# Copying the turned probabilities of memory pairs with VectorE in place of ScalarE, in layer 0's prompt attention

## The chip, the core and the metric

One core of a Trainium2 chip runs the whole program. Its engines are TensorE (PE in the profile, with its weight loads as PEld), VectorE (DVE), ScalarE (ACT), GpSimd (POOL) and SyncE (SP, which here only issues the loads of weights). Each engine works through its own list of instructions in order; they wait for each other through semaphores. The metric is the time of one execution in microseconds (us).

## What is computed

The reference is one step of a two-layer decoder for a prompt of 1,024 tokens and a sample group of 8 x 4 tokens. What matters here is the attention of layer 0 over the prompt, which has two parts that share one output projection:

```
# sliding window: 12 query heads on 4 key/value heads, blocks of 128 queries, 256 keys (own block and the one before)
s = einsum(q, k) * 64**-0.5 - slope * dist         # masked outside the window
m = max(max(s), sink);  e = exp(s - m)
p = e / (sum(e) + exp(sink - m));  o = einsum(p, v)
# memory: 4 heads, every query on 256 memory tokens, no bias
s = einsum(xq, mk) * 64**-0.5
p = softmax(s);  xo = einsum(p, mv)
x = x + concat([o, xo]) @ w_out
```

Layer 1 has the same memory attention, and a gated mixer in place of the window.

## The kernel before

All activations lie in SBUF with features on partitions and the 1,056 tokens along the free dimension. Most of the program is projections in which each fp32 product is split into three (lines 449 to 451); weights stream in through `raw`, are split by ScalarE and GpSimd, and TensorE is never long without work there.

The change concerns `prompt_attention(0)`, a stage of its own between the sample attention and the output projection. Its work is a list of 48 items: for each of 8 blocks of 128 queries four window items, called g0 to g3 here (three heads each, on a shared key/value head), and two memory items, m0 and m1 (a pair of heads each). An item passes through these steps:

- scores (PE, L645): 3 or 2 matmuls of 256 keys into two PSUM banks, which alternate between items.
- top (DVE): for a window item, three bias additions that also copy the scores to `s_exp` (L1424), a maximum (L1430) and two tiny operations on the sink (L1433, L1436); for a memory item only a maximum straight from PSUM (L1440).
- exps (ACT, L1014 and L1017): the exponentials with their sums.
- scale: the reciprocal of the sum on DVE (L1449 and L1452, or L1454), then a multiplication on POOL (L419).
- turn (PE, L659): transposes of the probabilities into PSUM banks 4 and 5, 6 or 4 of 128 x 128.
- take: one copy of these from PSUM to `p_t` in SBUF, 768 columns wide for a window item (384 in block 0) and 512 for a memory item. It is recorded at L850, the line of the helper `scopy` on ScalarE.
- values (PE, L672 for window items, L678 for memory items): the products with v.
- high (ACT, L850) and low (DVE, L1460): the split of the output into its high part `h_hi` and the rest, `h_lo`.

What sets the order is the loop `for n in range(...)` that each engine has, with LAG = 3. In turn n, TensorE does scores(n), turn(n-3), values(n-4). ScalarE does take(n-3), high(n-4), exps(n). VectorE does low(n-5), top(n), scale(n-1). Banks 4 and 5 are not doubled: turn(n) waits until take(n-1) is done (`pturned_taken`). `p_t` is doubled: take(n) waits for values(n-2) (`pv`). So m0 and m1 of a block are turned, and their probabilities taken, in the turns that do the scores of g1 and g2 of the next block; the last two are taken after the last scores. The wait that ties the engines most closely is this one, in TensorE's `turn`:

```
pe.wait_ge(m["normed"], n + 1)
if n >= 1:
    pe.wait_ge(m["pturned_taken"], n)
```

Of the kernel before, what the change touches and what calls it, by code (L numbers as in the profile page):

```python
# [64 lines left out]
LAG = 3  # L65
# [44 lines left out]
def swa_items(layer):  # L110

    out = []
    for b in range(NB):
        if layer == 0:
            out += [("swa", b, g) for g in range(A_KV)]
        out += [("mem", b, p) for p in range(2)]
    return out


def hybrid_step(nc, d, o, slopes):  # L120
    ctx = ExitStack()
    with ctx:
# [8 lines left out]
        def put(name, shape, dt=F32):  # L131
            t = nc.alloc_sbuf_tensor_at(name, shape, dt, offset=cursor[0])
            cursor[0] += size(shape)
            return t
# [80 lines left out]
        p_t = put("p_t", [P, 2, 2 * 3 * P])  # L215
# [45 lines left out]
        def banks(b, n, width):  # L261
            return ps[:, b:b + n, :].rearrange("p b n -> p (b n)")[:, 0:width]
# [585 lines left out]
        def _(act):  # L848
            def scopy(out, in_):
                return act.activation(out, in_, ACT.Copy)  # L850
# [145 lines left out]
            def prompt_attention(l):  # L996
                m = mx[l]
                items = swa_items(l)
                se, pt, st = (s_exp, p_t, stat) if l == 0 else (s_exp1, p_t1, stat1)
                N = len(items)  # L1000
                if l == 0:

                    act.wait_ge(outs, 16 * n_out[0])

                def exps(n):
                    kind, b, g = items[n]
                    act.wait_ge(m["ready"], n + 1)
                    if kind == "mem" and n >= RING:
                        act.wait_ge(m["pturned"], n - RING + 1)
                    w = BLOCK if kind == "swa" and b == 0 else 256  # L1010
                    for hh in range(3 if kind == "swa" else 2):
                        dst = se[:, n % RING, hh * 256:hh * 256 + w]
                        src = dst if kind == "swa" else ps[:, 2 * (n % 2) + hh, 0:w]
                        ins = act.activation(dst, src, ACT.Exp, bias=st[:, n % 4, 1, hh:hh + 1],  # L1014
                                             accum_out=st[:, n % 4, 2, hh:hh + 1])
                    if kind == "swa":
                        ins = act.activation(st[:, n % 4, 4, :], st[:, n % 4, 3, :], ACT.Exp)  # L1017
                    ins.then_inc(m["exped"], 1)

                def take(n):  # L1020
                    kind, b, g = items[n]
                    nh = 3 if kind == "swa" else 2
                    w = nh * P * (1 if kind == "swa" and b == 0 else 2)
                    act.wait_ge(m["pturned"], n + 1)
                    if n >= 2:
                        act.wait_ge(m["pv"], n - 1)
                    scopy(pt[:, n % 2, 0:w], banks(4, 2, 768)[:, 0:w]).then_inc(m["pturned_taken"], 1)

                def high(n):
                    act.wait_ge(m["pv"], n + 1)  # L1030
                    dst, src = o_view(items[n], n, h_hi)
                    scopy(dst, src).then_inc(m["o_cut"], 1)

                for n in range(N + LAG + 2):
                    if 0 <= n - LAG < N:
                        take(n - LAG)
                    if 0 <= n - LAG - 1 < N:
                        high(n - LAG - 1)
                    if n < N:
                        exps(n)  # L1040
                    if l == 1 and n < NB + 1:

                        w, t0 = (TS, 0) if n == 0 else (BLOCK, TS + (n - 1) * BLOCK)
                        act.wait_ge(m["gate_mult"], n + 1)
                        scopy(h_hi[:, 0:6, t0:t0 + w], z[:, 0:6, t0:t0 + w]).then_inc(m["gate_cut"], 1)
# [75 lines left out]
            for l in range(2):  # L1121
                m = mx[l]
# [63 lines left out]
                if l == 1:  # L1186
                    for n in range(NB + 1):
# [4 lines left out]
                        scopy(vn_tok[0:w, n % 2, :], banks(0, 2, 768)[0:w]).then_inc(m["gate_taken"], 1)  # L1192
                sample_attention(l)
                prompt_attention(l)

                if l == 1:
# [44 lines left out]
        def _(dve):  # L1241
# [45 lines left out]
            for r in range(N_MEMU):  # L1287
                l, q = r // 4, r % 4
# [115 lines left out]
            def prompt_attention(l):  # L1404
                m = mx[l]
                items = swa_items(l)
                se, st = (s_exp, stat) if l == 0 else (s_exp1, stat1)
                N = len(items)
                sums = [0, 0]

                def top(n):
                    kind, b, g = items[n]
                    s4 = n % 4
                    dve.wait_ge(m["scored"], n + 1)
                    out = banks(2 * (n % 2), 2, 768)
                    if n >= 4:
                        dve.wait_ge(m["normed"], n - 3)
                    if kind == "swa":
                        if n >= RING:

                            dve.wait_ge(m["pturned"], n - RING + 1)
                        w, nd0 = (BLOCK, BLOCK) if b == 0 else (256, 0)
                        for j in range(3):
                            STT(out=se[:, n % RING, j * 256:j * 256 + w], in0=nd_p[:, nd0:nd0 + w],  # L1424
                                scalar=float(slopes[3 * g + j]), in1=out[:, j * 256:j * 256 + w],
                                op0=ALU.mult, op1=ALU.add).then_inc(m["biased"], 1)
                        sums[0] += 3
                        dve.wait_ge(m["biased"], sums[0])
                        src = se[:, n % RING, :].rearrange("p (j k) -> p j k", j=3)[:, :, 0:w]
                        dve.tensor_reduce(st[:, s4, 0, :], src, AX, ALU.max, negate=True).then_inc(m["maxed"], 1)  # L1430
                        sums[1] += 1
                        dve.wait_ge(m["maxed"], sums[1])
                        TT(st[:, s4, 1, :], st[:, s4, 0, :], nsink_p[:, 3 * g:3 * g + 3], ALU.min) \  # L1433
                            .then_inc(m["maxed2"], 1)
                        dve.wait_ge(m["maxed2"], sums[1])
                        TT(st[:, s4, 3, :], st[:, s4, 1, :], nsink_p[:, 3 * g:3 * g + 3], ALU.subtract) \  # L1436
                            .then_inc(m["ready"], 1)
                    else:
                        src = ps[:, 2 * (n % 2):2 * (n % 2) + 2, 0:256]
                        dve.tensor_reduce(st[:, s4, 1, 0:2], src, AX, ALU.max, negate=True).then_inc(m["ready"], 1)  # L1440

                swas = [0]

                def scale(n):
                    kind, b, g = items[n]
                    s4 = n % 4
                    dve.wait_ge(m["exped"], n + 1)
                    if kind == "swa":
                        TT(st[:, s4, 0, :], st[:, s4, 2, :], st[:, s4, 4, :], ALU.add).then_inc(m["summed"], 1)  # L1449
                        swas[0] += 1  # L1450
                        dve.wait_ge(m["summed"], swas[0])
                        dve.reciprocal(st[:, s4, 5, :], st[:, s4, 0, :]).then_inc(m["recip"], 1)  # L1452
                    else:
                        dve.reciprocal(st[:, s4, 5, 0:2], st[:, s4, 2, 0:2]).then_inc(m["recip"], 1)  # L1454

                def low(n):
                    dve.wait_ge(m["o_cut"], n + 1)
                    dst, src = o_view(items[n], n, h_lo)
                    hi, _ = o_view(items[n], n, h_hi)
                    TT(dst, src, hi.bitcast(F32), ALU.subtract).then_inc(m["o_done"], 1)  # L1460

                for n in range(N + LAG + 2):
                    if 0 <= n - LAG - 2 < N:
                        low(n - LAG - 2)
                    if n < N:
                        top(n)
                    if 0 <= n - 1 < N:
                        scale(n - 1)
                    if l == 1 and 1 <= n < NB + 2:

                        w, t0 = (TS, 0) if n == 1 else (BLOCK, TS + (n - 2) * BLOCK)
                        dve.wait_ge(m["gate_cut"], n)
                        TT(h_lo[:, 0:6, t0:t0 + w], z[:, 0:6, t0:t0 + w], h_hi[:, 0:6, t0:t0 + w].bitcast(F32),
                           ALU.subtract).then_inc(m["gate_done"], 1)
# [129 lines left out]
            for l in range(2):  # L1604
                m = mx[l]
# [229 lines left out]
```

## Time and profile before

| | before |
|---|---|
| time, median of 3 runs | 2440.69 us |
| the three runs | 2440.69, 2440.61, 2445.96 us |
| span of the profiled execution | 2437.8 us |
| prompt attention of layer 0 in it | about 290 to 441.5 us |
| PE busy | 2364.8 us, 97% |
| DVE busy | 1152.4 us, 47% |
| ACT busy | 674.6 us, 28% |
| POOL busy | 596.1 us, 24% |

The span is what the profiler saw between the first and the last instruction; the time of a run has a few us around it (the median is 2.9 us above the span; the profiled execution's own time is not listed apart). Matmuls are pipelined and their ends are modelled, so that a busy TensorE is one that has something in flight. In a timeline row the first number is the start in us from the beginning of the span, the second the length; the square bracket at the end tells how long the engine sat idle before, and who released it.

### The profile page before, as it was taken

How to read it: one execution, taken by the hardware profiler on the slowest of the kernel's cores; microseconds unless marked ns; L12 is line 12 of the kernel's file. 1: busy time of each engine (PE TensorE's matmuls, PEld its weight loads, DVE VectorE, ACT ScalarE, POOL GpSimd, SP SyncE). 2: the span in 40 equal slices, each digit the busy share in tenths (PEclk: the TensorE clock that was granted, in tenths of full speed). 3: DMA queues.
4: the chain of work that ended last, by engine and by line, in shares of the span. 5: the costliest groups of instructions: out<-in, count | busy, mean ns of one | idle time of the engine just before them, and what ended most of it. 6: DMA issues, size and time to landing. Idle time of an engine off the chain costs nothing.

```text
span 2437.8 us, 37784 instructions
## 1 busy us (share of the span) xinstructions
PE 2364.8 (97%) x14538; PEld 2238.3 (92%) x14538; DVE 1152.4 (47%) x2144; ACT 674.6 (28%) x1247; POOL 596.1 (24%) x413
## 2 busy tenths in 40 slices
PE   5999999999999999999999998899999999999999
PEld 5898755899999999999999997699999999999999
DVE  7213377245454455554455133415555445445554
ACT  6211277242211112222225222514222221112221
POOL 3111033342212122222224121333222221212221
PEclk9998799999999999999999998899999999999999
DMA  5213000111111111111111112011111111111112
GB/s 202 86 44 139 5 1 1 29 44 61 44 43 35 42 47 48 52 52 52 43 35 51 44 44 95 4 43 35 52 53 52 52 43 43 35 42 44 50 52 84
DMA packets 36288, 123.29 MB, mean 51 GB/s; under 512 B 5264, under 2 KB 9968, under 8 KB 34896
## 3 DMA queue, kind: packets, MB, share of 16 engines
q1 hardware_dynamic: 26208, 95.43, 12.7%
q10 hardware_dynamic: 10000, 26.76, 2.9%
q8 instruction: 54, 0.88, 0.2%
q14 instruction: 26, 0.21, 0.0%
HBM read 115.57 MB, written 8.63 MB: 51 GB/s over the span
## 4 chain that ended last, share of the span: by engine, by line
PE 87%; DVE 5%; issue 4%; ACT 2%; POOL 1%; ACTq 0%; DMA 0%; DVEq 0%; POOLq 0%
PE ps L449 26%; PE ps L450 26%; PE ps L451 25%; PE ps L645 2%; DVE h_lo L1258 2%; PE ps L672 2%; PE ps L578 1%; PE ps L659 1%; PE ps L610 1%; ACT s_exp L1014 1%; DVE z L1645 1%; PE ps L722 1%; PE ps L560 1%; ACT p_t L850 0%; DVE s_exp L1424 0%
## 5 line engine op out<-in xcount | busy, mean ns | idle before, releaser
L449 PE MATMUL ps<-h_hi,w_hi 128*128 128x352 f32 x3120 | 1012.7, 325 | 14.9 <-DVE h_lo L1258 5.6
L450 PE MATMUL ps<-h_lo,w_hi 128*128 128x352 f32 x3120 | 1001.5, 321 | 0.0
L451 PE MATMUL ps<-h_hi,w_lo 128*128 128x352 f32 x3120 | 1000.7, 321 | 0.0
L356 POOL TENSOR_TENSOR w_lo<-raw,w_hi 128x1024 fp32r<-128x1024 f32 x138 | 345.1, 2502 | 1497.3 <-ACT w_hi L850 1497.3
L449 PEld LDWEIGHTS ps<-h_hi,w_hi 128*128 128x128 f32 x3120 | 586.3, 188 | 36.5 <-issue 22.3
L450 PEld LDWEIGHTS ps<-h_lo,w_hi 128*128 128x128 f32 x3120 | 587.2, 188 | 0.0
L451 PEld LDWEIGHTS ps<-h_hi,w_lo 128*128 128x128 f32 x3120 | 585.9, 188 | 0.0
L1565 DVE TENSOR_TENSOR x<-x,ps 128x352 f32<-128x352 f32 x528 | 270.7, 519 | 173.9 <-PE ps L451 173.1
L449 PE MATMUL ps<-g_hi,d_hi 128*128 128x352 f32 x1056 | 340.4, 322 | 3.5 <-DVE g_lo L1558 3.5
L450 PE MATMUL ps<-g_lo,d_hi 128*128 128x352 f32 x1056 | 339.9, 322 | 0.0
L451 PE MATMUL ps<-g_hi,d_lo 128*128 128x352 f32 x1056 | 339.7, 322 | 0.0
L850 ACT ACTIVATE w_hi<-raw 128x1024 fp32r<-128x1024 f32 x138 | 144.8, 1051 | 443.5 <-PE ps L451 430.2
L449 PEld LDWEIGHTS ps<-g_hi,d_hi 128*128 128x128 f32 x1056 | 198.3, 188 | 4.0 <-issue 4.0
L451 PEld LDWEIGHTS ps<-g_hi,d_lo 128*128 128x128 f32 x1056 | 198.7, 188 | 0.0
L450 PEld LDWEIGHTS ps<-g_lo,d_hi 128*128 128x128 f32 x1056 | 198.4, 188 | 0.0
L850 ACT ACTIVATE g_hi<-g_f 128x352 fp32r<-128x352 f32 x132 | 64.1, 498 | 443.5 <-DVE g_f L1552 443.5
L1619 DVE TENSOR_TENSOR z<-ps,rb 128x352 f32<-128x352 f32 x78 | 40.1, 523 | 236.0 <-PE ps L451 217.4
L1491 DVE SCALAR_TENSOR_TENSOR c_buf<-a_buf,conv_c,c_buf 128x1024 f32<-128x1024 f32 x88 | 150.3, 1708 | 2.8
L1552 DVE TENSOR_TENSOR g_f<-c_buf,ps 128x352 f32<-128x352 f32 x132 | 66.4, 518 | 165.4 <-PE ps L451 163.2
L1538 DVE TENSOR_TENSOR a_buf<-ps,rb 128x352 f32<-128x352 f32 x88 | 45.8, 524 | 208.0 <-PE ps L451 208.0
L419 POOL TENSOR_SCALAR s_exp<-s_exp,stat 128x256 f32<-128x256 f32 (+1 forms) x160 | 78.7, 507 | 223.7 <-DVE stat L1452 122.0
L356 POOL TENSOR_TENSOR d_lo<-raw,d_hi 128x1024 fp32r<-128x1024 f32 x44 | 106.6, 2422 | 67.9 <-ACT d_hi L850 67.9
(175 smaller groups left out, 1897.0 us busy)
## 6 DMA issues: line engine op xcount, KB each, us to landing
raw<-in_w SPq DMA_DIRECT2D x182, 512.0 KB, 3.6
x<-in_x_t ACTq DMA_DIRECT2D x4, 1056.0 KB, 10.0
out_y<-x ACTq DMA_DIRECT2D x8, 528.0 KB
s_mk<-in_s_mk ACTq DMA_DIRECT2D x2, 2048.0 KB, 9.5
s_mv<-in_s_mv ACTq DMA_DIRECT2D x2, 2048.0 KB, 14.6
mem_x<-in_mem_t ACTq DMA_DIRECT2D x1, 1024.0 KB, 7.0
s_k<-in_s_k ACTq DMA_DIRECT2D x2, 512.0 KB, 4.4
s_v<-in_s_v ACTq DMA_DIRECT2D x1, 1024.0 KB, 17.1
```

The source lines that it names most:

```text
L356: pool.tensor_tensor(lo, raw[:, slot], hi.bitcast(F32), ALU.subtract).then_inc(prepped, 1)
L419: ins = pool.tensor_scalar(v, v, st[:, n % 4, 5, hh:hh + 1], 1.0, ALU.mult, ALU.mult)
L449: pe.matmul(out, a, hi_x(k), start=(first and n == 0), stop=False)
L450: pe.matmul(out, a, lo_x(k), start=False, stop=False)
L451: ins = pe.matmul(out, b, hi_x(k), start=False, stop=(last and n == len(ks) - 1))
L645: mm = pe.matmul(out[:, hh * step:hh * step + w], lhs, rhs, start=True, stop=True)
L672: mm = pe.matmul(ps[64 * half:64 * half + 64, 6 + n % 2, 0:384], v_tok[:, b - len(kcs) + 1 + kc, g * HD:(g + 1) * HD], pt[:, n % 2, kc * 3 ...
L850: return act.activation(out, in_, ACT.Copy)
L1258: STT(out=h_lo[:, k, cs], in0=x[:, k, cs], scalar=gain[:, g_i, k:k + 1], in1=h_hi[:, k, cs].bitcast(F32), op0=ALU.mult, op1=ALU.subtract). ...
L1491: ins = STT(out=cp, in0=ab[:, 48 + j:48 + j + SEQ], scalar=cc[:, j:j + 1], in1=cp, op0=ALU.mult, op1=ALU.add)
L1552: TT(g_f[:, c * CH:(c + 1) * CH], c_buf[:, s, c * CH:(c + 1) * CH], ps[:, 3 + c, 0:CH], ALU.mult).then_inc(freed[1], 1)
L1565: TT(xx, xx, ps[:, 3 + (q + 1) % 5, 0:CH], ALU.add).then_inc(dn_added, 1)
```

## The change

In layer 0 the 16 takes of memory items leave ScalarE and are done by VectorE with `tensor_copy`, with the same two waits and the same signal. Those of window items, and all of layer 1, stay. ScalarE's loop skips them; VectorE's loop has them as the last step of a turn: low(n-5), top(n), scale(n-1), take(n-3).

```diff
@@ ScalarE, prompt_attention
                 for n in range(N + LAG + 2):
-                    if 0 <= n - LAG < N:
+                    if 0 <= n - LAG < N and (l == 1 or items[n - LAG][0] == "swa"):
                         take(n - LAG)
@@ VectorE, prompt_attention
+                def take(n):
+                    dve.wait_ge(m["pturned"], n + 1)
+                    if n >= 2:
+                        dve.wait_ge(m["pv"], n - 1)
+                    dve.tensor_copy(p_t[:, n % 2, 0:512], banks(4, 2, 768)[:, 0:512]).then_inc(m["pturned_taken"], 1)
...
                         top(n)
                     if 0 <= n - 1 < N:
                         scale(n - 1)
+                    if l == 0 and 0 <= n - LAG < N and items[n - LAG][0] == "mem":
+                        take(n - LAG)
```

VectorE's order in a block, before: top of g1 (four rows), the scale of g0 (L1449, L1452), then low of the g3 of the block before (L1460), and the beginning of top of g2.

```order
L1424 SCALAR_TENSOR_TENSOR s_exp<-nd_p,ps 128x256 x3
L1430 TENSOR_REDUCE stat<-s_exp 128x3
L1433 TENSOR_TENSOR stat<-stat,nsink_p 128x3
L1436 TENSOR_TENSOR stat<-stat,nsink_p 128x3
L1449 TENSOR_TENSOR stat<-stat 128x3
L1452 RECIPROCAL stat<-stat 128x3
L1460 TENSOR_TENSOR h_lo<-ps,h_hi 64x3x128
L1424 SCALAR_TENSOR_TENSOR s_exp<-nd_p,ps 128x256 x3
L1430 TENSOR_REDUCE stat<-s_exp 128x3
L1433 TENSOR_TENSOR stat<-stat,nsink_p 128x3
```

The same place of VectorE in the changed program, where line numbers behind the new function are higher by 6 (L1430 is L1424 of before, L1458 is L1452, L1466 is L1460) and L1415 is the new copy:

```order
L1430 SCALAR_TENSOR_TENSOR s_exp<-nd_p,ps 128x256 x3
L1436 TENSOR_REDUCE stat<-s_exp 128x3
L1439 TENSOR_TENSOR stat<-stat,nsink_p 128x3
L1442 TENSOR_TENSOR stat<-stat,nsink_p 128x3
L1455 TENSOR_TENSOR stat<-stat 128x3
L1458 RECIPROCAL stat<-stat 128x3
L1415 COPY p_t<-ps 128x512
L1466 TENSOR_TENSOR h_lo<-ps,h_hi 64x3x128
L1430 SCALAR_TENSOR_TENSOR s_exp<-nd_p,ps 128x256 x3
```

The copy for m0 stands between the reciprocal of g0 and low of g3; the copy for m1 stands one turn later in the same way, between the reciprocal of g1 and low of m0. ScalarE at the same place, before and then changed, where p_t<-ps is a take and h_hi<-ps a high:

```order
L1017 ACTIVATE stat<-stat 128x3
L850 ACTIVATE p_t<-ps 128x512
L850 ACTIVATE h_hi<-ps 64x3x128
L1014 ACTIVATE s_exp,stat<-s_exp,stat 128x256 x3
L1017 ACTIVATE stat<-stat 128x3
L850 ACTIVATE p_t<-ps 128x512
L850 ACTIVATE h_hi<-ps 128x128
```

```order
L1017 ACTIVATE stat<-stat 128x3
L850 ACTIVATE h_hi<-ps 64x3x128
L1014 ACTIVATE s_exp,stat<-s_exp,stat 128x256 x3
L1017 ACTIVATE stat<-stat 128x3
L850 ACTIVATE h_hi<-ps 128x128
```

On ScalarE both takes are gone, and what stood around them now stands side by side. TensorE's order is the same in both programs.

## Rows read from the trace of the kernel before

**Rows 1.** The page, part 1: each engine's busy time, share of the span, instructions.

```profile
PE 2364.8 (97%) x14538; PEld 2238.3 (92%) x14538; DVE 1152.4 (47%) x2144; ACT 674.6 (28%) x1247; POOL 596.1 (24%) x413
```

**Rows 2.** Busy time by stage: layer 0's prompt attention, and two us of layer 1's.

```profile
core 0: us, PE busy (x) PEld busy (x) DVE busy (x) ACT busy (x) POOL busy (x), PEclk, DMA share, GB/s
292.00:440.00 148.00, 144.57 (x730) 83.88 (x732) 109.32 (x328) 115.71 (x383) 57.90 (x128) 0.97 0.00 1
1552.00:1554.00 2.00, 1.56 (x16) 0.86 (x14) 1.74 (x4) 2.00 (x8) 1.57 (x2) 1.00 0.05 12
```

**Rows 3.** Costliest groups, shapes apart, from 290 to 442 us.

```profile
L1440 DVE TENSOR_REDUCE stat<-ps 128x2 f32<-128x512 f32 x16 | 10.8, 678 | 0.1
...
L850 ACT ACTIVATE p_t<-ps 128x512 f32<-128x512 f32 x16 | 9.5, 596 | 0.7 <-PE ps L659 0.3
```

**Rows 4.** The same view over the whole span: VectorE reads of PSUM and SBUF.

```profile
L1619 DVE TENSOR_TENSOR z<-ps,rb 128x352 f32<-128x352 f32 x78 | 40.1, 523 | 236.0 <-PE ps L451 217.4 <-ACT rb L850 18.7
...
L1396 DVE COPY o_s<-ps 64x32 f32<-64x32 f32 x8 | 1.5, 189 | 25.0 <-PE ps L610 24.9
...
L1320 DVE COPY s_k<-z 128x256 f32<-128x256 f32 x2 | 0.5, 289 | 0.0
```

**Rows 5.** Timeline, prompt block 3, 363 to 375 us (start, length, engine, instruction).

```profile
363.63 1.08 DVE L1424 SCALAR_TENSOR_TENSOR s_exp<-nd_p,ps 128x256 f32<-128x256 f32 x3 [0.42 <-PE ps L645]
...
366.20 0.18 DVE L1452 RECIPROCAL stat<-stat 128x3 f32<-128x3 f32 x1
366.41 0.56 DVE L1460 TENSOR_TENSOR h_lo<-ps,h_hi 64x384 fp32r<-64x384 f32 x1
...
367.03 0.66 PE L659 MATMUL ps<-ident,s_exp 128*128 128x128 f32 x4
...
367.14 1.08 DVE L1424 SCALAR_TENSOR_TENSOR s_exp<-nd_p,ps 128x256 f32<-128x256 f32 x3 [0.17 <-PE ps L645]
...
367.86 0.60 ACT L850 ACTIVATE p_t<-ps 128x512 f32<-128x512 f32 x1
...
369.63 0.51 ACT L1014 ACTIVATE s_exp<-s_exp,stat 128x256 f32<-128x256 f32 x1 [1.00 <-DVE stat L1436]
...
369.70 0.87 PE L659 MATMUL ps<-ident,s_exp 128*128 128x128 f32 x6
369.71 0.18 DVE L1452 RECIPROCAL stat<-stat 128x3 f32<-128x3 f32 x1
369.80 0.26 DVE L1460 TENSOR_TENSOR h_lo<-ps,h_hi 128x128 fp32r<-128x128 f32 x1
...
369.98 1.07 DVE L1424 SCALAR_TENSOR_TENSOR s_exp<-nd_p,ps 128x256 f32<-128x256 f32 x3
...
372.16 0.84 PE L659 MATMUL ps<-ident,s_exp 128*128 128x128 f32 x6 [0.36 <-ACT p_t L850]
...
374.06 0.79 ACT L850 ACTIVATE p_t<-ps 128x768 f32<-128x768 f32 x1
...
375.00 0.88 PE L659 MATMUL ps<-ident,s_exp 128*128 128x128 f32 x6
```

**Rows 6.** Timeline, prompt block 1, 309 to 319 us.

```profile
309.54 0.18 DVE L1452 RECIPROCAL stat<-stat 128x3 f32<-128x3 f32 x1
...
310.34 1.08 DVE L1424 SCALAR_TENSOR_TENSOR s_exp<-nd_p,ps 128x256 f32<-128x256 f32 x3
...
313.18 1.07 DVE L1424 SCALAR_TENSOR_TENSOR s_exp<-nd_p,ps 128x256 f32<-128x256 f32 x3
...
318.20 0.87 PE L659 MATMUL ps<-ident,s_exp 128*128 128x128 f32 x6
```

**Rows 7.** Timeline, end of the stage and the first matmul of the output projection.

```profile
439.13 0.56 DVE L1460 TENSOR_TENSOR h_lo<-ps,h_hi 64x384 fp32r<-64x384 f32 x1 [1.69 <-ACT h_hi L850]
439.20 0.60 ACT L850 ACTIVATE p_t<-ps 128x512 f32<-128x512 f32 x1
...
441.52 0.42 PE L449 MATMUL ps<-h_hi,w_hi 128*128 128x352 f32 x1 [1.01 <-DVE h_lo L1460]
```

**Rows 8.** Line 659, transposes on TensorE: duration in ns, minimum/median/maximum.

```profile
L659 PE MATMUL ps<-ident,s_exp x308: 272/273/474, 295.1 to 1573.7; 128*128 128x128 f32 x154
```

## The prediction

> **What bounds the kernel now.** Begin with the engines' shares [rows 1]: TensorE has work in flight for 97% of the span, so a change can shorten the program only where TensorE waits, and lengthens it where it makes TensorE wait. Next the stage [rows 2]: in the 148 us of layer 0's prompt attention TensorE is busy for 144.6, ScalarE for 115.7, VectorE for 109.3. Neither helper is full, and ScalarE is the fuller one; by these sums alone the move looks harmless. The sums don't say who is late at which moment, so the timeline of one block comes next [rows 5]. The blocks repeat every 18.93 us from block 2 to block 7; the rows are of block 4. What to see in them:
>
> - TensorE turns m0's successor m1 at 367.03, g0 at 369.70, g1 at 372.16 and g2 at 375.00. Its only idle time of note is 0.36 us before 372.16, for ScalarE's take of g0. Before 375.00 it is on the edge too: ScalarE's take of g1 ends at 374.06 + 0.79 = 374.85, and the turn starts 0.15 later.
> - ScalarE takes m1 at 367.86, then still sits idle for 1.00 us before its exponentials of g2 at 369.63, until VectorE has finished top of g2.
> - VectorE idles 0.42 us before top of g1 (363.63) and 0.17 us before top of g2 (367.14), both times for TensorE's scores. From 367.14 on it goes through top of g2, the reciprocal at 369.71, low of m0 at 369.80 and top of g3 at 369.98 without a pause.
>
> So in the middle of a block the chain runs VectorE (top), ScalarE (exponentials, then the take behind them), TensorE (turn). VectorE leads it. In this stretch the engine that receives the copies is the one that is late, and the one that gives them up is waiting for it.
>
> **What is removed.** Sixteen ScalarE copies of 596 ns [rows 3], 9.5 us of work. Both of a block lie ahead of an idle time: exponentials of g2 can't start before VectorE's top, whatever ScalarE has to do before. Removing 0.60 us from in front of 1.00 us of waiting gains nothing. If it did gain, only TensorE's 0.36 us per block could be won back.
>
> **What is added: the length of one copy.** No row shows VectorE copying 512 fp32 columns from PSUM. The nearest: a maximum over 512 columns from PSUM takes 678 ns [rows 3]; an addition with a 352-column PSUM operand takes 523 ns and a copy of 32 columns 189 ns [rows 4], a slope of (523 - 189) / 320 = 1.044 ns a column, which gives 189 + 480 x 1.044 = 690 ns. The other end: the copy from SBUF to SBUF of 256 columns takes 289 ns [rows 4], that is 100 ns for 224 columns more than 32, or 0.45 ns each; at such a rate 512 columns would take 189 + 480 x 0.45 = 405 ns. I take 690, since it rests on two kinds of PSUM reads and the maximum lies within 12 ns of it, and keep 405 and, for waits that no row prices, 760 as the ends.
>
> The Trainium skill bears on this choice ("VectorE: DVE Perf Modes"). Its tier table allows `tensor_copy` up to two results a cycle from PSUM, which would put it near the short end, while its section "Why PSUM operands drop a tier" says one for fp32, since VectorE has one PSUM read port; no row here shows a wide copy from PSUM. Its cycle table, 120 + 512 cycles at 0.96 GHz, gives an estimate of 658 ns, and the sum below would come out 0.5 us lower by it.
>
> **What is added: the shift, in a steady block.** Take m0: it is ready (turned before 365), so it starts when VectorE gets to it. In the rows an instruction can start 0.09 us after the start of a reciprocal (369.71, 369.80), so the copy runs from 366.20 + 0.09 = 366.29 to 366.98. TensorE's turn of m1 needs it and moves from 367.03 to some 367.1, which is covered by waits further on. Low of g3 moves from 366.41 to 367.01 (it writes the other half of the partitions, and at 366.41 it too started only once its forerunner had ended), ends at 367.57, and top of g2 starts at 367.60 in place of 367.14: **0.46 later**, the copy less the small idle times in front of it.
>
> Take m1: VectorE reaches it after top of g2 and the reciprocal, at 369.80 + 0.46 = 370.26, and ends at 370.95. ScalarE did it at 367.86. TensorE's turn of g0 needs it, and moves from 369.70 to 370.95 + 0.15 = 371.10, **1.40 later**; this is the new wait, and queued behind it on TensorE stand values of m1, the scores of m0 and the turn of g1. Low of m0 and top of g3 follow the copy; as an independent instruction starts 0.08 before its forerunner's end (low of m0 ends at 370.06, the next starts at 369.98), the copy costs 0.61 in the queue, and top of g3 moves by 0.46 + 0.61 = **1.07**, to 371.05.
>
> What of it reaches the end of the block? Along TensorE: from the turn of g0 to that of g1 it has 372.16 - 369.70 - 0.36 = 2.10 of work and from there to the turn of g2 2.84, so that the turn of g2 could stand at 371.10 + 2.10 + 2.84 = 376.04, 1.04 later. The take of g0 doesn't add to this: it is ready 0.9 after the turn began and is over before 373.2. Along VectorE and ScalarE: top of g3, its exponentials and the take of g1 keep their distances, so the take ends at 374.85 + 1.07 = 375.92 and the turn stands at 376.07, **1.07 later**. The later of the two holds. Behind the turn of g2 comes TensorE's stretch without waits, and at the next block's top of g1 VectorE waits for TensorE again (0.42 us), so that nothing is left over or piled up. POOL's multiplications move with the reciprocals and are over before their turns, as now. No DMA is issued in the stage's loop, and the weight buffers are full while it runs.
>
> **The first block and the end.** Block 1 is the first to do this, and in it VectorE has no idle time ahead of top of g2: it starts at 310.34, right behind low [rows 6]. The copy for m0 would run from 309.63 to 310.32, low starts at 310.35, 0.60 late, and top of g3 (313.18) moves by 0.60 + 0.61 = 1.21, with it the turn of g2 at 318.20. Blocks 2 to 7 are six steady ones. At the end, low of the last g3 ends at 439.69 and ScalarE's take of the last m1 runs from 439.20 to 439.80 [rows 7]; VectorE can start it at 439.72 only and ends at 440.41, 0.61 later, and the output projection's first matmul (441.52) waits for values, high and low behind it.
>
> **The sum.** 6 x 1.07 + 1.21 + 0.61 = 8.24 us. All of it shifts a program that is TensorE's work from there on. The span goes from 2437.8 to 2446.0, and with the 2.9 us by which the median of the runs lies above the span, the median from 2440.7 to **2448.9**, 0.34% more.
>
> **The rivals.**
>
> *The copy is short.* It decides in the same place: with 0.405 in place of 0.690 the shift of top of g3 is 2 x 0.285 = 0.57 less in each of seven blocks, and the end 0.29 less, together 4.3 us less: 2444.6 us, which is not slower by 0.3%. The point from which it decides: 0.3% is 7.3 us (about what a measurement of this kernel can tell from no change), which needs a copy of about 0.63 us, since each 0.01 us costs 0.15. For it speaks the SBUF copy's rate [rows 4], against it every wide read of PSUM. Chance 0.12.
>
> *ScalarE was the one that was late.* If the copies hid in VectorE's idle time and ScalarE's relief counted, TensorE's waits for the take of g0 would go: 0.36 x 7, with the first block's about 3 us. That gives 2437.7 us, which is faster but within 0.3%. Against it stands the 1.00 us that ScalarE waits for VectorE [rows 5]. Chance 0.03.
>
> *The clock of TensorE falls.* It is granted in full here (0.97 of 2.4 GHz over the stage), and the new wait leaves TensorE without work for 1.3 us in every block. At the lower level a transpose takes 474 ns in place of 273 [rows 8], 1.74 times; one block of 18.6 us of work there would cost up to 14 us, 2463 us in all. Against it: in layer 1's attention TensorE is busy for 1.56 us of 2, and the clock stays full [rows 2]. Chance 0.02.
>
> *The mechanism holds with another size.* Should VectorE's two added waits cost 0.07 each (copy 0.76), it is 9.3 us; should the instructions overlap by 0.08 more at low of g3, 7.7 us. These are the bounds of my own case, 0.83.
>
> **How the numbers follow.** Of my own case's 0.83 I put 0.66 above 7.3 us, as its centre lies only 0.9 above. With the clock's 0.02, slower has 0.68. The rest of my case, the short copy and most of ScalarE's case make 0.30 for within 0.3%; faster keeps 0.02. The range leaves out the clock's case, the gain and a little of the short copy's side: 2444.6 to 2451.5, where 1.5 us at the upper end is for the spread between runs.
>
> **What would show it.** In the changed profile: the copy of `p_t` on VectorE 16 times at 0.69 us; TensorE idle some 1.3 us before one turn in each block, released by VectorE's copy, and no longer 0.36 for the take of g0; the blocks 20.0 us apart in place of 18.93; ScalarE's busy time 9.5 us lower and VectorE's 11 higher; the output projection starting at 449.8. I am wrong if the copy takes about 0.4, if the period stays at 18.9 (the copies hidden), or if the transposes of this stage show 474 ns.

## The result, and the profile after

The change makes the kernel slower: 2454.57 us against 2440.65, a ratio of 1.0056 with a 95% interval of 1.0042 to 1.0070, or 13.9 us. The prediction had 8.2 us and a range up to 2451.5, so the time came out later than the whole range: the direction is right and the size is not. (The two medians rest on four runs each; later runs of both kernels, below, spread more than these did.)

The span of the profiled execution is 2453.1 us, 15.3 more than before. The page's engine row (busy us, share of the span, instructions) answers to [rows 1]:

```profile
PE 2371.7 (97%) x14538; PEld 2244.5 (91%) x14538; DVE 1163.6 (47%) x2160; ACT 667.9 (27%) x1231; POOL 596.6 (24%) x413
```

VectorE has 16 instructions and 11.2 us more, ScalarE 16 and 6.7 us less. TensorE has the same instructions and 6.9 us more busy time, which is the first hint: no wait makes a matmul longer. ScalarE's busy time fell by less than the 9.5 us forecast because a copy overlaps its neighbours on the engine: the 0.60 us copy at 367.86 in [rows 5] still runs when ScalarE's next instruction starts at 368.36.

The timeline of block 3 answers to [rows 5], whose rows are of block 4, as the prediction says and not its caption; the steady blocks are alike (line numbers behind the new function are 6 higher, and the clock stayed full in block 3 of this profile):

```profile
351.06 1.08 DVE L1430 SCALAR_TENSOR_TENSOR s_exp<-nd_p,ps 128x256 f32<-128x256 f32 x3 [0.42 <-PE ps L645]
...
353.64 0.18 DVE L1458 RECIPROCAL stat<-stat 128x3 f32<-128x3 f32 x1
353.73 0.68 DVE L1415 COPY p_t<-ps 128x512 f32<-128x512 f32 x1
...
354.44 0.56 DVE L1466 TENSOR_TENSOR h_lo<-ps,h_hi 64x384 fp32r<-64x384 f32 x1
354.55 0.63 PE L659 MATMUL ps<-ident,s_exp 128*128 128x128 f32 x4
355.03 1.08 DVE L1430 SCALAR_TENSOR_TENSOR s_exp<-nd_p,ps 128x256 f32<-128x256 f32 x3
...
357.53 0.51 ACT L1014 ACTIVATE s_exp<-s_exp,stat 128x256 f32<-128x256 f32 x1 [1.42 <-DVE stat L1442]
...
357.69 0.68 DVE L1415 COPY p_t<-ps 128x512 f32<-128x512 f32 x1
358.29 0.28 DVE L1466 TENSOR_TENSOR h_lo<-ps,h_hi 128x128 fp32r<-128x128 f32 x1
358.48 1.07 DVE L1430 SCALAR_TENSOR_TENSOR s_exp<-nd_p,ps 128x256 f32<-128x256 f32 x3
358.52 0.84 PE L659 MATMUL ps<-ident,s_exp 128*128 128x128 f32 x6 [1.25 <-DVE p_t L1415]
```

Everything stands where the prediction put it. Counted from top of g1, top of g2 starts 3.97 us later, where it started 3.51 later before (+0.46); the turn of g0 starts at 7.46 in place of 6.07 (+1.39) behind an idle time of 1.25 us that VectorE's copy ends; top of g3 starts at 7.42 in place of 6.35 (+1.07). ScalarE's wait for top of g2 has grown from 1.00 to 1.42 us: its relief went into waiting.

One block later the same turn looks different. Timeline of block 4, the copy and TensorE behind it, then windows over the same time (columns: busy us and count, granted clock, DMA share, GB/s):

```profile
377.65 0.68 DVE L1415 COPY p_t<-ps 128x512 f32<-128x512 f32 x1
378.48 1.28 PE L659 MATMUL ps<-ident,s_exp 128*128 128x128 f32 x6 [1.25 <-DVE p_t L1415]
380.75 1.22 PE L645 MATMUL ps<-mem_k,z 64*128 64x256 f32 x4
```

```profile
376.00:378.00 2.00, 1.23 (x6) 1.00 0.00 0
378.00:380.00 2.00, 1.52 (x10) 0.68 0.04 12
380.00:382.00 2.00, 2.00 (x13) 0.50 0.00 0
382.00:384.00 2.00, 2.00 (x10) 0.96 0.00 0
```

The six transposes take 1.28 us in place of 0.84. Some 0.3 us into them the clock falls from 2.4 to 1.2 GHz and comes back 3.4 us later. What TensorE did before it fell: it stood idle for 1.25 us, and was busy before and after. The same happens in blocks 1, 4 and 6, and once more right after the stage, where TensorE had waited for the last copy (0.71 us) and, after 0.7 us of work, for the last high and low (1.01 us). With the tops of g1 as marks, the stage is:

| | before | after |
|---|---|---|
| first scores of the stage | 288.5 | 292.0 |
| from there to top of g0, block 1 | 15.6 | 14.8 |
| top of g1, block 1, to top of g1, block 2 | 18.77 | 21.39 |
| the same for blocks 2 to 6 | 18.93 or 18.94 | 19.97, 19.97, 21.41, 19.96, 21.38 |
| top of g1, block 7, to the output projection | 21.09 | 22.75 |
| first scores to the output projection | 153.0 | 164.5 |

The 15.3 us of the span are thus: 3.5 before the stage, where nothing was changed; 11.5 in the stage; 0.3 behind it (the output projection took 1.5 us more there, and the profile before had a stretch at 1.2 GHz of its own, from 561.4 us, that this one lacks). The 11.5 are 8.0 of added waiting (1.04 in each of six steady blocks, 1.2 in block 1, 0.6 at the end), 4.3 for three blocks that are 1.43 us longer, and 0.8 less before the first copy, as the clock there came back to its full level sooner after the stage's start.

### The profile page after: what moved, and what is told of

It is laid out like the page before. It is cut to its first block, busy times and chain, and to the rows that moved or that the text cites. A ratio compares the mean times of both kernels' runs of the same rounds, so it can differ in the third digit from the quotient of the medians.

```text
span 2453.1 us, 37784 instructions
## 1 busy us (share of the span) xinstructions
PE 2371.7 (97%) x14538; PEld 2244.5 (91%) x14538; DVE 1163.6 (47%) x2160; ACT 667.9 (27%) x1231; POOL 596.6 (24%) x413
## 4 chain that ended last, share of the span: by engine, by line
PE 86%; DVE 6%; issue 4%; ACT 2%; POOL 1%; ACTq 0%; DVEq 0%; POOLq 0%
PE ps L449 26%; PE ps L450 25%; PE ps L451 25%; DVE h_lo L1258 2%; PE ps L645 2%; PE ps L672 1%; PE ps L578 1%; PE ps L659 1%; PE ps L610 1%; DVE s_exp L1430 1%; DVE stat L1436 1%; DVE z L1653 1%; PE ps L722 1%; PE ps L560 1%; ACT s_exp L1014 0%
```

## Experiments

The questions: do the two copies make the 8.0 us, each in its place? What are the blocks with the lower clock, and the 3.5 us ahead of the stage?

**The kernel before and the changed kernel, again.** No edit.

> The kernel before, unchanged, for a second profile of it. In the profile after the change the stage begins 3.5 us later than in the one of before (292.0 against 288.5 us), though nothing in front of it is changed: TensorE's clock stood at its lower level over other stretches. Theory A (those stretches come with the program and return with it): the stage begins at 288.5 again, within 0.3 us, the same stretches show the lower clock, ratio to the kernel before 1.000. Theory B (they come by chance with each execution): the stage begins anywhere within some 3 us of that, and the lower clock lies elsewhere. In both the stage itself, first scores to first matmul of the output projection, takes 153.0 us within 1, with no lower clock after its first 14 us.

> The changed kernel, unchanged, for a second profile of it. In the first one the stage takes 164.5 us against 153.0 and shows three stretches of 3.4 us at the lower clock (from 317, 379 and 420 us), each of which made its block 1.4 us longer; my sum of waits had 8.2 us. Theory A (the stretches return with the program): the same three blocks, stage 164.5 us, start at 292.0. Theory B (the new wait opens the door to them, chance decides which blocks): again one to seven such stretches, in other blocks, stage 160 to 170 us. Theory C (they have nothing to do with the change): none, stage 161 us. In all, blocks without such a stretch are 19.97 us apart (18.93 before).

Before, again: median 2442.39 of 11 runs, ratio 1.0001 [0.9990, 1.0011]. The stage began at 291.6, not at 288.5, and took 152.2 us, its blocks 18.94 apart, with no lower clock in blocks 1 to 7. After, again: 2454.09 of 5 runs, ratio 1.0052 [1.0033, 1.0071]. The stage began at 289.6 and took 162.3 us; block 5 alone was longer (21.34), the others 19.94 to 19.97. Theory B holds and A falls: the stretches don't come with the program. The 3.5 us ahead of the stage are chance, and single times of either kernel spread by many us: 2438.7 to 2447.2 before, 2446.2 to 2459.0 after. The added waiting was the same in both profiles of the changed kernel.

**Half of the change.**

```diff
 # m0_only (m1_only with 0 and 1 exchanged)
-                    if 0 <= n - LAG < N and (l == 1 or items[n - LAG][0] == "swa"):
+                    if 0 <= n - LAG < N and (l == 1 or items[n - LAG][0] == "swa" or items[n - LAG][2] == 1):
                         take(n - LAG)          # ScalarE
...
-                    if l == 0 and 0 <= n - LAG < N and items[n - LAG][0] == "mem":
+                    if l == 0 and 0 <= n - LAG < N and items[n - LAG][0] == "mem" and items[n - LAG][2] == 0:
                         take(n - LAG)          # VectorE
```

> Half the change: only the copy of m0 goes to VectorE, m1's stays on ScalarE. By my sum of waits: top of g2 moves by 0.46 us in a steady block and the turn of g2 with it, 0.60 in block 1, nothing at the end: blocks 19.39 us apart, the stage longer by 0.60 + 6 x 0.46 = 3.4 us without any clock effect. TensorE's wait ahead of g0's turn (1.25 us with the whole change) isn't there; it has two short ones instead, below 0.9. If the lower clock comes with the long wait, there is none of it here in blocks 2 to 7, and the ratio is about 1.0014. If it has nothing to do with that wait, some blocks show it, 1.4 us each.

> The other half: only the copy of m1 goes to VectorE. It starts at once behind the reciprocal of g1: turn of g0 0.94 us late, top of g3 0.60 late and with it the turn of g2: blocks 19.53 us apart, the stage longer by 7 x 0.60 + 0.61 = 4.8 us without clock effect; TensorE waits about 0.9 us ahead of g0's turn. The two halves together (3.4 + 4.8) make the 8.2 of the whole change if the mechanism is additive. If a wait of 0.9 us is long enough for the lower clock, one or more blocks are 1.4 us longer in addition; if it takes the 1.25 of the whole change, none is.

Copy of m0 alone: blocks 19.39 apart, the stage behind top of g0 of block 1 at 140.8 us against 137.4 to 137.5 in the two profiles of before (+3.3), ratio 1.0008 [0.9996, 1.0020]. The copy of m1 alone: 19.51 apart, 142.15 (+4.7), ratio 1.0038 [1.0023, 1.0054]. 3.3 and 4.7 make the 8.0 of the whole. The turn that waits, in the timelines of m0_only and then of m1_only:

```profile
355.92 0.85 PE L659 MATMUL ps<-ident,s_exp 128*128 128x128 f32 x6 [0.75 <-ACT p_t L850]
```

```profile
315.77 0.68 DVE L1415 COPY p_t<-ps 128x512 f32<-128x512 f32 x1
316.60 0.85 PE L659 MATMUL ps<-ident,s_exp 128*128 128x128 f32 x6 [1.50 <-DVE p_t L1415]
...
355.63 0.85 PE L659 MATMUL ps<-ident,s_exp 128*128 128x128 f32 x6 [0.86 <-DVE p_t L1415]
```

With m0 alone it is g1's turn that waits, and for ScalarE: VectorE's delay has reached it by way of the exponentials. Neither profile shows a lower clock in blocks 1 to 7. But the times of m1_only lay 9 us above before, more than the 4.7 of its stage. So it was run again:

> The half with only m1's copy on VectorE, a second profile. Its first showed no lower clock in blocks 1 to 7 with waits of 0.9 us, and the stage was 4.7 us longer as worked out, but its times were 9 us above the kernel before. If waits of 0.9 us also let the clock fall in some executions, this one may show it, 1.4 us for each block; if they are too short, it shows none, the stage is 157.3 within 1 us, and what the times had more came from outside the stage.

This execution took 2457.99 us (span 2456.3), in a stage of 158.3. Block 1, where the wait is 1.50 us and not 0.86, was 20.80 long in place of 19.36, with the clock at 1.2 GHz for 3.4 us; the other six were 19.51. So the lower clock can follow this wait too. The rest of the execution's excess came from outside the stage: its span less the stage is 2298.0 us, where the two profiles of before have 2284.8 and 2286.8. Some 1.7 us of it are the output projection, in which the clock fell too, as in the changed kernel. The granted clock that is on record for every run points the same way. A mean clock lower by 0.001 is 0.2% of the span at 1.2 GHz in place of 2.4; if TensorE works through it, half of that time is lost, an estimated 2.4 us. The six runs of m1_only have a mean clock of 0.9772 against 0.9790 of the kernel before beside them, so an estimated 4.4 us, and with the 4.7 of the stage that is the 9 measured. Why the clock was lower, in both profiles mostly outside the stage, where the programs are alike, is not settled.

**TensorE kept busy while it waits.** The whole change, and:

```diff
                     pe.wait_ge(m["normed"], n + 1)
+                    if l == 0 and (kind, g) == ("swa", 0) and b >= 1:
+                        pe.wait_ge(m["o_done"], n - 2)
+                        for _ in range(9):
+                            pe.transpose(ps[:, 6 + (n - 1) % 2, 384:512], ident[:, :], ident[:, :])
                     if n >= 1:
                         pe.wait_ge(m["pturned_taken"], n)
```

> The whole change, and in blocks 1 to 7 TensorE does nine transposes of the identity (into a corner of a PSUM bank that nobody reads, 1.2 us in all) while it waits for VectorE's copy of m1 ahead of g0's turn. Theory B (the lower clock in these blocks comes from TensorE standing idle there): no stretch of lower clock in blocks 1 to 7, blocks 19.97 to 20.05 us apart, stage about 161 us (153 + 8.2), ratio to the kernel before about 1.0035, where the whole change measured 1.0052 and 1.0056. Rival C (the lower clock comes by chance whatever TensorE does): some blocks again 1.4 us longer, and the ratio is 1.005 or more.

The timeline of block 3, then TensorE's busy time and granted clock from block 1 to block 7 (start and end of the window, its length, busy us and count, clock, DMA share, GB/s); behind it the same window of the changed kernel:

```profile
357.21 1.20 PE L655 MATMUL ps<-ident 128*128 128x128 f32 x9
358.45 0.88 PE L663 MATMUL ps<-ident,s_exp 128*128 128x128 f32 x6
```

```profile
310.00:450.00 140.00, 138.03 (x734) 1.00 0.00 1
```

```profile
310.00:450.00 140.00, 130.22 (x654) 0.96 0.00 1
```

The wait is full of transposes and ends as late as before: blocks 19.95 to 19.97, all seven alike. The clock never fell, and the stage behind top of g0 of block 1 took 145.45 us, 8.0 more than before, the added waiting alone. The median, 2450.68 of 5 runs, lies 3.9 us below that of the changed kernel in the first comparison; the ratio, 1.0044 [1.0030, 1.0058], is higher than the 1.0035 expected, and its interval overlaps that of the changed kernel, so the time alone would not prove it. The profile speaks against rival C, which expected longer blocks: there are none. One profile is not much, since the changed kernel itself once had only one such block in seven; at its rate of 10 in 28 (below), none in seven would still come about once in 22 times, if each block were independent. The runs agree with it: the mean clock of the five is 0.9782 against 0.9788 of before, an estimated 1.5 us, where after_again has 0.9774 against 0.9790, 3.9 us. The profiled execution itself took 2454.77 us, 4 more than the median; what it had more lay outside the stage (2292.9 us).

**A wait of the same kind from ScalarE.** The kernel before, with no work moved to VectorE:

```diff
-                    if 0 <= n - LAG < N:
+                    late = l == 0 and 0 <= n - LAG < N and items[n - LAG][0] == "mem" and items[n - LAG][2] == 1
+                    if 0 <= n - LAG < N and not late:
                         take(n - LAG)
...
                     if n < N:
                         exps(n)
+                    if late:
+                        take(n - LAG)
```

> The kernel before, with all copies on ScalarE, but m1's copy done behind the exponentials of g2 and not ahead of them. VectorE's work is unchanged. TensorE's turn of g0 then waits until 371.3 + 0.6 + 0.15 = 372.07 in place of 369.70, an idle time of 2.4 us in one piece; behind it TensorE's own work gives the next turns 2.0 us late: blocks 20.9 us apart, the stage 14 us longer. Theory B (a long idle piece of TensorE lets the clock fall, whoever causes it): stretches of 3.4 us at the lower clock in most blocks, 1.4 us each, blocks of 22.3 us, the stage 14 + 1.4 x 4 to 7 = 20 to 24 us longer, ratio 1.008 to 1.010. Rival (VectorE's copy from PSUM is what the lower clock goes with): no such stretches, ratio 1.0057.

Timeline of one block, the turn of g0 behind its wait and, two steps on, the turn of g1; then the busy time and granted clock from block 1 to block 7:

```profile
385.31 0.84 PE L659 MATMUL ps<-ident,s_exp 128*128 128x128 f32 x6 [2.17 <-ACT p_t L850]
...
387.80 1.54 PE L659 MATMUL ps<-ident,s_exp 128*128 128x128 f32 x6
```

```profile
310.00:456.00 146.00, 130.16 (x615) 0.89 0.00 1
```

2472.14 us of 4 runs, ratio 1.0136 [1.0119, 1.0153]: the clock fell in every one of the seven blocks (22.2 to 23.7 us long, where waiting alone was expected to give 20.9), although no copy was on VectorE. The rival falls. It came out worse than theory B's numbers, 27 us of stage against 20 to 24, since in three blocks the lower clock lasted about 6.8 us and not 3.4.

**Two more profiles of the changed kernel.**

> The changed kernel once more, for a third profile. Profiles so far showed the lower clock in 3 and in 1 of blocks 1 to 7; the one with TensorE kept busy in the wait showed none. If chance decides in each execution whether the 1.25 us wait of a block lets the clock fall, this one shows between 1 and 5, in blocks of its own, each block then 21.4 us and the others 19.97; the stage is 161 + 1.4 for each.

> As after_third, a fourth profile: 1 to 5 stretches again, and the stage 161 us + 1.4 for each. If three and one had been the odd ones and most executions show none, then the clock isn't what my sum lacked, and the stage is 161.

Blocks 2, 5 and 7 in one (2454.43 us, stage 164.1), blocks 1, 3 and 6 in the other (2454.77 us, stage 164.8), three each, the undisturbed blocks 19.95 to 19.98. In the four profiles of the changed kernel the clock fell in 10 of 28 blocks, and in three of the four once more at the start of the output projection, which then took 103.5 us to the next stage in place of 102.0 to 102.2. The blocks of all profiles in the old order of items:

| TensorE's longest wait in a block | blocks seen | clock fell in |
|---|---|---|
| 0.36 us, 0.99 in block 1 (before, twice) | 14 | 0 |
| 0.75 us, 0.80 in block 1 (m0_only) | 7 | 0 |
| 0.86 us (m1_only, twice, blocks 2 to 7) | 12 | 0 |
| 1.50 us (m1_only, twice, block 1) | 2 | 1 |
| 1.25 us (whole change, four times) | 28 | 10 |
| 1.25 us, filled with transposes | 7 | 0 |
| 2.2 to 2.8 us (scalar_late) | 7 | 7 |

The start of the output projection is a second place. Where TensorE waited 0.71 to 0.87 us for the last take and, 0.7 us of work later, 1.0 us more (whole change four times, m1_only, m1_again, filled, scalar_late), the clock fell in 4 of 8 profiles; with the 1.0 us wait alone (before twice, m0_only), in 0 of 3. No run was made to separate the two waits.

The length of the idle piece doesn't decide alone. Elsewhere in the 13 profiles, in the projections, TensorE has single idle pieces that no run here changed: after pieces of 1.32 us the clock fell in 3 of 26, after 1.76 us in 0 of 26, after 2.3 us in 9 of 23. So the table's numbers hold for this stage, and what else decides stays open.

**Where the copies fall.** The same six items of a block, with the memory items apart:

```diff
-            out += [("swa", b, g) for g in range(A_KV)]
-        out += [("mem", b, p) for p in range(2)]
+            out += [("swa", b, 0), ("swa", b, 1), ("mem", b, 0), ("swa", b, 2), ("swa", b, 3), ("mem", b, 1)]
+        else:
+            out += [("mem", b, p) for p in range(2)]
```

> The kernel before with the six items of a block in another order, g0 g1 m0 g2 g3 m1 in place of g0 g1 g2 g3 m0 m1. All copies on ScalarE. In the old order two short turns of TensorE follow each other while VectorE has two long tops, and TensorE idles 0.36 us a block for the take behind them. With the memory items apart this idle time should go: blocks 18.6 us apart in place of 18.93, the stage 2.5 us shorter, ratio 0.999. If the chain VectorE, ScalarE, TensorE is too long for one short turn also, TensorE idles twice for up to 0.3, and the blocks stay at 18.9.

> The same order g0 g1 m0 g2 g3 m1 with the change: VectorE copies for m0 and m1. Each copy then falls into a turn of VectorE whose top is the short one of a memory item (0.68 us in place of 2.5). If the cost of the change lies in where the copies fall (my account), they are hidden: blocks within 0.2 us of those of the same order without the change, about 18.6 to 18.8, no lower clock, ratio 0.999 to 1.001. If VectorE's total work is what costs, the blocks are 1.0 us longer than without the change, as in the old order, and the ratio is 1.003.

Without the change: blocks 18.54 apart, the stage 151.3 us, ratio 0.9994 [0.9982, 1.0005]. With the change: blocks 18.54 apart as well, the stage 151.8 us, ratio 1.0004 [0.9992, 1.0016]. The same sixteen copies on VectorE, as long as before (677 ns), cost nothing in a steady block. The clock fell in none of blocks 1 to 7 of either profile. The timeline shows why the copies are hidden; the first row is the top of a memory item, the second the copy, the third the turn that needs it, which starts with no idle time before it:

```profile
373.64 0.67 DVE L1447 TENSOR_REDUCE stat<-ps 128x2 f32<-128x512 f32 x1
...
375.02 0.68 DVE L1416 COPY p_t<-ps 128x512 f32<-128x512 f32 x1
...
376.68 0.88 PE L660 MATMUL ps<-ident,s_exp 128*128 128x128 f32 x6
```

The new order without the change is 1 to 2 us better in the stage than the kernel before (153.0 and 152.2), less than the 2.5 expected and too little for the times to show: its interval holds 1. In it the move to VectorE adds 0.5 us to the stage, all of it ahead of block 2, which the times can't show either.

## Why the prediction was wrong: the waits were right, the clock's term was missing

- **The length of the copy.** 690 ns were taken, 672 to 691 measured, 677 in the mean. The short end, 405, is out. By the Trainium skill ("VectorE: DVE Perf Modes", "Why PSUM operands drop a tier") fp32 from PSUM moves one element a cycle. The trace agrees: from 189 ns for 32 columns to 677 for 512 it is 1.02 ns a column, and a cycle at the 0.96 GHz of that page is 1.04. The estimate of 658 ns from its cycle table is 19 below the measured mean.
- **The shift in a steady block.** 1.07 predicted, 1.04 measured in all undisturbed blocks; top of g2 +0.46 and top of g3 +1.07 as worked out; the wait ahead of g0's turn 1.3 predicted, 1.25 measured. The halves, 0.46 and 0.60 by the same sum, came out at 0.45 and 0.58.
- **First block and end.** 1.21 and 0.61 predicted, 1.17 (after_again) and 0.61 measured. The sum of the waiting: 8.2 predicted, 8.0 measured, in four profiles of the whole change and in the filled one.
- **What ScalarE gains.** Nothing, as said: its busy time fell by 6.7 us, its wait ahead of the exponentials of g2 grew.
- **The step that failed is the rival "the clock of TensorE falls".** The sum has only waits in it and no term for the clock, and the rival that has one, with its place and its cause named, was given a chance of 0.02 and a price of up to 14 us for one block. Instead it is the common case: one to three of the seven blocks in each profile, at 1.4 us each, and three times of four the start of the output projection at 1.5. That is 2.5 blocks in the mean, 3.6 us, and 1.1 for the projection: 4.7 us on top of 8.0, together 12.7 of the 13.9 measured. The sign that the prediction named for this case, slow transposes, is there as well: in the stretches they took mostly 421 ns and up to 477, where at the full clock none of the stage behind block 0 takes more than 332. The remaining 1.2 us are less than what the parts outside the stage vary by from one execution to the next (2282.2 to 2288.6 us for span less stage, in the four profiles of the changed kernel).
- **Why it was put aside wrongly.** The argument was that layer 1's attention is busy for 1.56 us of 2 and keeps its clock [rows 2]. There the idle time comes in pieces below 0.5 us; here the busy share is higher, but the idle time is one piece of 1.25. Shares were compared where pieces should have been. The trace of the kernel before had the contrary case outside the stage: in a projection, after one idle piece of 1.32 us with dense work on both sides, the clock fell at 561.38 and the matmuls took 0.49 us in place of 0.32 for 3.4 us.

```profile
561.20 0.47 PE L449 MATMUL ps<-h_hi,w_hi 128*128 128x352 f32 x1 [1.32 <-DVE a_buf L1535]
...
563.51 0.49 PE L451 MATMUL ps<-h_hi,w_lo 128*128 128x352 f32 x1
...
566.03 0.32 PE L451 MATMUL ps<-h_hi,w_lo 128*128 128x352 f32 x1
```

The Trainium skill ("TensorE: Matmul & The Clock Gate", "What's actually happening") says that activity releases a throttle which is the default, and that the monitor runs freely, without regard to a kernel's start. The trace agrees with the second: the blocks in which the clock falls differ in each of four executions.

- **The range.** Its upper end had 1.5 us for the spread between runs, read from three times, two of which agreed to 0.1 us. Eleven runs of the same kernel on one chip spread over 8.4 us.
- **The rival "ScalarE was late"** is out: without ScalarE's two copies the block got longer. That the copies would hide in VectorE's idle time is true in another order of items only (spread_after).

## What to carry to other kernels

Before work is moved to the less loaded engine, find in the timeline which engine leads the chain at the moment where the work would fall: here 0.68 us cost 0.45 to 0.58 each behind a long step of VectorE and nothing behind a short one. And where TensorE is otherwise saturated, a new wait of more than a microsecond in one piece is to be priced twice, for itself and for the clock that may fall behind it. Look through the trace before for idle pieces of that length and what the clock did after them; busy shares don't tell, and one profile doesn't either, since chance decides in each execution where it falls.

## What the runs showed of the hardware

- In this stage a single idle piece of 1.25 us of TensorE, with dense work on both sides, was followed by 3.4 us at 1.2 GHz in 10 of 28 cases, one of 2.2 us or more by 3.4 or 6.8 us in 7 of 7, pieces of 0.86 us or less in 0 of 31 (0.99 us: 0 of 2). In the projections the same profiles have 3 of 26 for 1.32 us, 0 of 26 for 1.76 and 9 of 23 for 2.3, so this is no rule of length alone. A stretch of 3.4 us costs 1.4 us in the attention and 1.5 to 1.7 in the output projection.
- Outside the stage the clock's stretches move from execution to execution too. The first scores of the stage came between 287.6 and 293.5 us in programs that are alike up to there. The five runs of after_again go in order of their mean clock, from 2446.2 us at 0.981 to 2459.0 at 0.974, and the median of a few runs of this kernel is uncertain by some us.
- VectorE copied 128 x 512 fp32 values from PSUM to SBUF in 672 to 691 ns, 677 in the mean; ScalarE took 596 ns for the same copy.
